# Sums of weight blocks for the last MLP, made by transfers within memory during the mixer

## What is computed

```python
def sq_relu_mlp(x, w_in, w_out):
    return jnp.square(jax.nn.relu(x @ w_in)) @ w_out

for layer in range(DEPTH):                       # DEPTH = 2
    hn = rms_norm(h, norm_mix_pre[layer])
    m = mixer_ab(hn, ...) if layer % 2 == 0 else mixer_ret(hn, ...)
    h = h + rms_norm(m, norm_mix_post[layer])
    f = sq_relu_mlp(rms_norm(h, norm_ffn_pre[layer]), ffn_w_in[layer], ffn_w_out[layer])
    h = h + rms_norm(f, norm_ffn_post[layer])
```

## Time and profile before

| | |
|---|---|
| median of 3 runs | 1478.39 us (1477.74 to 1479.36) |
| span of the profiled execution | 1476.8 us |
| median less span | 1.6 us |
| TensorE busy | 1436.1 us, 97% |
| VectorE busy | 921.3 us, 62% |
| GpSimd busy | 87.2 us, 6% |
| moved by the DMA engines | 160.21 MB |

### The profile page before, as it was taken

One profiled execution on the slowest core, in us unless ns is written; L12 is line 12 of the kernel. 1 busy time (PEld: TensorE's weight loads), 2 busy tenths in 40 slices (PEclk: granted clock), 3 DMA queues, 4 the chain that ended last, 5 costly groups with the idle time before them and its releaser, 6 DMA issues.

```text
span 1476.8 us, 22066 instructions
## 1 busy us (share of the span) xinstructions
PE 1436.1 (97%) x9650; PEld 1183.2 (80%) x9650; DVE 921.3 (62%) x1200; ACT 538.7 (36%) x632; POOL 87.2 (6%) x89
## 2 busy tenths in 40 slices
PE   9999999998999999998999999999998999999997
PEld 6778777776888888887888888888887788888786
DVE  7768676667655565554665445355447776868654
ACT  7455454533312221223343332332434433433322
POOL 0000000012010100001200000000003000000000
PEclk9999999998999999999899999999998999999999
DMA  5211111101573644631212222222130352434332
GB/s 187 73 36 59 50 59 45 59 30 35 209 270 141 229 175 175 235 110 62 86 58 88 83 86 86 83 89 86 58 114 29 123 191 86 171 115 165 134 112 59
DMA packets 30623, 160.21 MB, mean 108 GB/s; under 512 B 2816, under 2 KB 6912, under 8 KB 15552
## 3 DMA queue, kind: packets, MB, share of 16 engines
q1 hardware_dynamic: 23456, 130.73, 24.4%
q0 software_dynamic: 7072, 28.08, 5.1%
HBM read 144.12 MB, written 14.68 MB: 108 GB/s over the span
## 4 chain that ended last, share of the span: by engine, by line
PE 89%; DVE 6%; ACT 2%; issue 1%; DMA 1%; POOL 1%; DVEq 0%; POOLq 0%
PE bank L388 20%; PE bank L394 20%; PE bank L391 20%; PE bank L691 2%; PE bank L694 2%; PE bank L695 2%; PE bank L1684 2%; PE bank L1681 2%; PE bank L1678 2%; PE bank L996 2%; PE bank L402 1%; PE bank L1003 1%; DVE WL L346 1%; PE bank L593 1%; PE bank L589 1%
## 5 line engine op out<-in xcount | busy, mean ns | idle before, releaser
L388 PE MATMUL bank<-XH,WH 128*128 128x512 f32 x944 | 379.2, 402 | 16.1 <-DVE XL L481 12.6
L394 PE MATMUL bank<-XH,WL 128*128 128x512 f32 x944 | 371.6, 394 | 0.0
L391 PE MATMUL bank<-XL,WH 128*128 128x512 f32 x944 | 371.6, 394 | 0.0
L346 DVE TENSOR_TENSOR WL<-raw,WH 128x2048 fp32r<-128x2048 f32 (+1 forms) x99 | 222.2, 2246 | 148.1 <-ACT WH L340 148.1
L340 ACT ACTIVATE WH<-raw 128x2048 fp32r<-128x2048 f32 (+1 forms) x99 | 185.3, 1873 | 195.5 <-DMA raw<-weights 195.3
L388 PEld LDWEIGHTS bank<-XH,WH 128*128 128x128 f32 x944 | 179.8, 190 | 60.3 <-issue 20.8
L394 PEld LDWEIGHTS bank<-XH,WL 128*128 128x128 f32 x944 | 179.6, 190 | 38.7
L391 PEld LDWEIGHTS bank<-XL,WH 128*128 128x128 f32 x944 | 179.7, 190 | 38.0 <-issue 1.9
L847 ACT ACTIVATE AH<-relu 128x512 fp32r<-128x512 f32 (+1 forms) x64 | 37.9, 592 | 209.1 <-DVE relu L876 209.1
L388 PE MATMUL bank<-AH,WH 128*128 128x512 f32 x256 | 99.7, 389 | 0.0
L394 PE MATMUL bank<-AH,WL 128*128 128x512 f32 x256 | 99.6, 389 | 0.0
(11 more groups left out here) (360 smaller groups left out, 2339.8 us busy)
## 6 DMA issues: line engine op xcount, KB each, us to landing
raw<-weights SPq DMA_DIRECT2D x104, 1024.0 KB, 4.8
block<-weights POOLq DMA_DIRECT2D x12, 1024.0 KB, 5.5
sums_of_blocks<-block POOLq DMA_DIRECT2D x12, 1024.0 KB, 5.4
raw<-sums_of_blocks SPq DMA_DIRECT2D x12, 1024.0 KB, 4.8
raw<-weights SPq DMA_DIRECT2D x8, 512.0 KB, 4.8
h<-x_fm SPq DMA_DIRECT2D x4, 512.0 KB, 7.9
out_tm<-h SPq DMA_DIRECT2D x8, 256.0 KB, 2.6
rc<-ret_const POOLq DMA_DIRECT2D x1, 1536.0 KB, 7.4
```

Of the source, the lines that this page charges most:

```text
L346: nc.vector.tensor_tensor(WL[i][:, :n], raw[i][:, :n], WH[i][:, :n], ALU.subtract).then_inc(S("w_lo"), 1)
L388: mm = pe.matmul(bank[b][:], wh, xh, start=(k == 0), stop=False)
L391: mm = pe.matmul(bank[b][:], wh, xl, start=False, stop=False)
L394: mm = pe.matmul(bank[b][:], wl, xh, start=False, stop=(k == len(xs) - 1))
```

## The change

The sums are no longer made by VectorE in the first MLP. GpSimd makes them with transfers from memory to memory: a plain copy of a block, or a transfer that adds its source to what stands at its destination. Since these only add, the sums are taken with other signs (all plus), and the minus signs go into the sums of the activations and into `ADDENDS`. For each of the three quarters there are eight transfers of 1 MB: S0 = b11, S0 += b12, S2 = b12, S2 += b22, S3 = S2, S3 += b11, S1 = S3, S1 += b21. Each waits until the one before has landed. The 24 are spread over the chunk phases of the four pairs, six in each, behind GpSimd's two additions. In the last MLP two operations of each activation sum become `scalar_tensor_tensor` in place of `tensor_tensor`. The wait of SyncE's queue before the first chunk of the last MLP now counts the new transfers.

```diff
@@ seven_dve @@
-        ADDENDS = (((0, 0, 1),), ((0, 0, 1),), ((1, 0, -1),), ((1, 1, 1),), ((0, 1, 1),), ((0, 1, 1),), ((1, 0, 1), (1, 1, 1)))
+        ADDENDS = (((0, 0, 1),), ((0, 0, 1),), ((1, 0, 1),), ((1, 1, -1),), ((0, 1, -1),), ((0, 1, -1),), ((1, 0, 1), (1, 1, -1)))
@@ activation_sums @@
-            nc.vector.tensor_tensor(S_both[:, 0, :], a21, a22, ALU.add).then_inc(S("s_step"), 1)
+            nc.vector.tensor_tensor(S_both[:, 0, :], a22, a21, ALU.subtract).then_inc(S("s_step"), 1)
             nc.vector.tensor_tensor(S_both[:, 2, :], a11, a21, ALU.subtract).then_inc(S("s_step"), 1)
             dve.wait_ge(S("s_step"), 4 * n + 1)
-            nc.vector.tensor_tensor(S_both[:, 1, :], S_both[:, 0, :], a11, ALU.subtract).then_inc(S("s_step"), 1)
+            nc.vector.scalar_tensor_tensor(S_both[:, 1, :], S_both[:, 0, :], -1.0, a11, ALU.mult, ALU.subtract).then_inc(S("s_step"), 1)
             dve.wait_ge(S("s_step"), 4 * n + 3)
-            nc.vector.tensor_tensor(S_both[:, 3, :], a12, S_both[:, 1, :], ALU.subtract).then_inc(S("s_step"), 1)
+            nc.vector.scalar_tensor_tensor(S_both[:, 3, :], a12, -1.0, S_both[:, 1, :], ALU.mult, ALU.subtract).then_inc(S("s_step"), 1)
-        def weight_sums(pool):
...
-        def weight_sums_dve(dve, n):
...
+        WEIGHT_SUMS = tuple((q, to, k) for q in range(SEVEN) for to, k in ((0, 0), (0, 2), (2, 2), (2, 3), (3, None), (3, 0), (1, None), (1, 1)))
+
+        def weight_sum_step(pool, n):
+            q, to, k = WEIGHT_SUMS[n]
+            if n:
+                pool.wait_ge(S("sums_moved"), 16 * n)
+            at, to_sum = FFN1_CHUNK + 8 * q + 4, sums_of_blocks[q, to]
+            if k is None:
+                pool.dma_start(to_sum, sums_of_blocks[q, 2 if to == 3 else 3]).then_inc(S("sums_moved"), 16)
+            elif n % 8 in (0, 2):
+                pool.dma_start(to_sum, weights[at + k]).then_inc(S("sums_moved"), 16)
+            else:
+                pool.dma_start(to_sum, weights[at + k], accum_op=ALU.add, max_dma_last_dim=4 * CHUNK).then_inc(S("sums_moved"), 16)
@@ ffn_dve @@
-                    if not layer and q < SEVEN and j in (9, 11, 13, 15):
-                        weight_sums_dve(dve, 4 * q + j // 2 - 4)
@@ chunks_pool @@
             nc.gpsimd.tensor_tensor(chunked(W[4]), chunked(W[4]), table(K_EYE2), ALU.add).then_inc(S("e1"), 1)
+            for n in range(6 * p, 6 * p + 6):
+                weight_sum_step(pool, n)
@@ sync @@
                 if c == FFN1_CHUNK:
-                    sync.wait_ge(S("sums_stored"), 16 * SEVEN * PIECES)
+                    sync.wait_ge(S("sums_moved"), 16 * 8 * SEVEN)
@@ gpsimd @@
                 if m == 1:
-                    weight_sums(pool)
+                    pool.wait_ge(S("a_lo"), 2)
                     pool.dma_start(rc[:], ret_const).then_inc(S("rc_loaded"), 16)
```

More of the change, by code:

```diff
@@ L52 @@
 HALF = T // 2
-PIECES = CHUNK // T
 V_NORM = 0
@@ L235, in trunk_kernel @@
         S_both = nc.alloc_sbuf_tensor_at("S_both", [P, 4, HALF], F32, offset=ffn.at - 4 * D)
-        blocks_at = ffn.at - 4 * D - 16 * 2 * T
-        block = [nc.alloc_sbuf_tensor_at(f"block{i}", [P, 4, T], F32, offset=blocks_at + i * 16 * T) for i in range(2)]
         uT = nc.alloc_sbuf_tensor_at("uT", [P, TT, D], F32, offset=start)
```

## The result

The changed kernel takes 1500.97 us (median, 1499.54 to 1505.17), beside 1478.07 for the kernel before on the same chip: 1.0162 of it, with a 95% interval of 1.0145 to 1.0179, or 22.9 us more. The forecast was 1498.7. The profiled execution took 1499.54 us, its span is 1497.8, 21.0 more than before.

What follows compares the result with a forecast made beforehand. TensorE, busy 97% of the span, was taken to bound the kernel. Terms 0 + 20 + 0 + 0 + 0.3 = 20.3 us, added to 1478.4, gave 1498.7 us, with an 8-in-10 range of 1477 to 1526.

Steps and rivals of the forecast that it cites:

- (1): First MLP: removing 48 vector operations and 24 transfers gives 0 us, since TensorE has no idle time there.
- (2): Chunk phases: TensorE's instruction packets wait until the transfer in progress drains from their DMA engine, stalling TensorE; 20 us.
- The stretch that was to grow by about 5 us: First chunk phase, stretch 63:101 of the trace, predicted to grow by about 5 us through TensorE's issue stalls.
- The formula: Chunk phases: mean stall per packet is (B - s)²/2 over the cycle, B the busy stretch, s the slack, 1 or 2 us.
- The cycles: GpSimd's transfers in the chunk phases: copy 5.3 us with engines busy 3.2, accumulate 8.0 with 6, together 13.3 us.
- (3): GpSimd's work behind its transfer waits: five transfers take 32 us, hidden with 12 us to spare in the last pair; 0.
- (4): Weight loads beside a transfer: a 3 us delay would still be covered by ScalarE's 4.39 us of idleness; 0.
- (5): Last MLP activation sums: two of four operations change form on VectorE, six on the path before a TensorE wait; +0.3 us.
- (6): SyncE's queue wait before the last MLP's first chunk: its transfers end near 320 instead of 615; 0.
- Rival B: Chunk phases: packets pass between a transfer's pieces, so only +0.3 us is left, 1478.7 us; chance 0.22.
- Rival C: Mixer: slow accumulates make GpSimd late for the last pair's sum, so the norm waits; 1521 to 1531 us; chance 0.14.
- Rival D: First MLP or a phase behind it gains by the missing transfers, at most tenths of a microsecond; 1478; chance 0.04.

Runs made afterwards that it cites:

- e1_none: The changed kernel without its 24 transfers, the last MLP loading plain blocks of weights in place of the sums: 1477.15 us, ratio 0.9997 to the kernel before.
- e2_first_mlp: The changed kernel with all its 24 transfers moved from the chunk phases into the first MLP: 1478.11 us, ratio 1.0009 to the kernel before.
- e6_copies_8k: e4_copies with each copy cut into 8 KB pieces, eight per DMA engine in place of one of 64 KB: 1522.74 us, ratio 1.0284 to the kernel before.
- e10_fronts: The changed kernel with nine transfers in the fronts of the second to fourth pairs and 15 in the first MLP: 1477.86 us, ratio 1.0002 to the kernel before.
- e4_copies: The changed kernel with each of its 24 transfers made a plain 1 MB copy, same places: 1523.78 us, ratio 1.0319 to the kernel before.
- e5_accumulates: The changed kernel with each of its 24 transfers made a 1 MB accumulate in 8 KB pieces: 1527.07 us, ratio 1.0321 to the kernel before.

## Why the prediction was right

The forecast of 1498.7 lies 2.3 us below the time. By its parts:

- **(1) First MLP, 0:** right. 222 matmuls in 50 us as in the earlier trace rows, and `e1_none` and `e2_first_mlp` find nothing to gain.
- **(2) Instruction packets wait for the transfer, +20:** the mechanism is right in the main, and the main cost: packets wait for transfers, and the gaps with "issue" end 2.2 to 2.7 us behind the start of a packet. "Until the transfer in progress has drained" is right beside copies, but of the eight packets that start during an accumulate six get in before any engine has done its part, and five of the eleven gaps of over 0.4 us in the chunk phases, 9.6 of their 17.2 us, follow such packets. The sum is only half right. The idleness is 14.4 us, below the 20; the rest is the clock, 7 us in the profiled execution and 10 by the mean of four, which the sum had no term for. That the total came out near is luck: two errors of opposite sign. The stretch that was to grow by about 5 us grew by 10.8 (the four pairs: 10.8, 4.2, 2.0 and 9.1). The formula failed in "a packet asked for at a random moment": in the copies the packets fall into step with the transfers, one to each. At half the size it asked for 1 to 4 us and the run gave 25. The forecast held at the one point for which it was made, and would have misled on any variant.
- **The cycles:** copy 5.3 us predicted, 5.6 to 7.8 measured (engines busy 3.7 to 4.6, and once 5.9, against 3.2); accumulate 8.0 predicted, 8.2 to 9.4 measured (5.6 to 6.8 against 6). Both a little low.
- **(3) GpSimd, 0:** right. With the longer cycles, five transfers take 34 to 37 us in place of 32, and the last pair's sum still waits 18 us for ScalarE.
- **(4), (5), (6):** too small to be seen. `e1_none` bounds (1) and (5) together at -2.5 to +1.6 us, and `e2_first_mlp`, which keeps SyncE's wait, bounds them and (6) at -0.7 to +3.2. For (4), no gap of TensorE of over 0.4 us in the four phases of the changed kernel is released by anything but "issue".
- **Rival B, no cost:** out, by 22.9 us. It leaned on the rule of the Trainium skill that has each DMA engine go round its queues packet by packet, which I read as a switch after each piece. That section ("DMA: Bandwidth & Descriptors", on queues, rings and completion order) also says that such a packet is some 9 to 17 descriptors, drained whole before a switch. Read so, eight pieces of 8 KB for each engine are about one packet, and `e6_copies_8k` agrees: the loss of the copies is 42 us with them and 47 without. Read so, the rule speaks for the forecast. The accumulates of 1 MB, also eight pieces for each engine, agree less: most instruction packets beside them get in before the end. The rival's other support, that GpSimd's transfers are cut in smaller pieces than SyncE's loads, is true of the kernel before (4 KB against 8) but not of the change, whose copies have 64 KB pieces and whose accumulates have 8.
- **Rival C, GpSimd late,** would have needed an accumulate of 14 us. **Rival D, faster,** is out with `e1_none`.

## What to carry to other kernels

Look at which stretches eat instructions fast (many small matmuls) and keep large transfers out of them: here the same 24 MB cost 23 us in the chunk phases and nothing in the first MLP, or with 9 of them in the fronts. (These are GpSimd's transfers; that a load of SyncE does the same rests on the one stall of the earlier trace rows.) Where one must stand there, make it short or let it stand alone: 128 KB at a time, or one copy in a phase, cost some 3 us in all. When estimating a stall of TensorE, ask for two terms, the stall and the clock behind it, and ask what the stall before it was: a second one 8 us later cost three times the first.

## What the runs showed of the hardware

- A copy within memory holds back TensorE's instruction packets until its part on the engine is done, 3.1 to 3.7 us for 1 MB, in 64 KB pieces and in 8 KB pieces alike. An accumulate of 1 MB lets one in 3.4 to 4.9 us behind its start or holds it to its end. TensorE resumes 2.2 to 2.8 us behind the packet's start.
- Four stalls of 2.6 to 2.9 us cost 12 us; eight, in pairs 8 to 10 us of work apart, cost 50 us, with no transfer about. The granted clock stood at 0.50 for nearly 14 us behind the second of a pair in the first phase, and for 17 in the next two.
- The clock can differ between executions with the same gaps. `e1_none` and `e2_first_mlp` have the same idle pieces of TensorE up to 85 us (the largest 0.69 us at 73.37 and 0.45 at 81.4); the first stays at 1.00, the second has 0.50 for 10 us from 84.7. `e10_fronts`, with nothing of its own in the first chunk phase, has 0.87 over it:

```profile
63.00:101.00 38.00, 35.36 (x847) 29.63 (x844) 20.57 (x34) 20.14 (x29) 2.51 (x2) 0.87 0.04 12
```

- A copy of 1 MB within memory keeps the engines busy for 3.7 to 4.6 us, first piece to last (once 5.9), and lands 5.4 us after its issue (median of `e4_copies`); an accumulate for 5.6 to 6.8, landing in 8.1 to 8.2 (medians of `e5_accumulates` and the changed kernel).
